# Layer 0 of a two-part transformer kernel: one gather of 8 KB rows in place of two gathers of 4 KB rows, over six places

## The reference, cut to what matters

```
def one(args):                      # a block of 128 tokens
    hh, ee, gg = args               # h, expert indices [128,128], gates [128,128]
    a = jnp.einsum("tkd,td->tk", peer_down[ee], hh)
    act = gg * jax.nn.gelu(a)
    return jnp.einsum("tk,tkd->td", act, peer_up[ee])
```

## Time and profile before

| | |
|---|---|
| median of 3 runs | 3811.63 us (3804.46 to 3811.77) |
| profiled execution, its own time | 3813.63 us |
| its span, first to last instruction | 3811.8 us |
| PE / DVE / ACT / POOL busy | 80% / 64% / 25% / 32% |
| bytes moved by DMA | 1156.88 MB, mean 304 GB/s |
| gathers (queue q0) | 805.39 MB |

### The profile page before, as it was taken

One profiled execution on the slowest core, in us unless ns is written; L12 is line 12 of the kernel. 1 busy time (PEld: TensorE's weight loads), 2 busy tenths in 40 slices (PEclk: granted clock), 3 DMA queues, 4 the chain that ended last, 5 costly groups with the idle time before them and its releaser, 6 DMA issues.

```text
span 3811.8 us, 42583 instructions
## 1 busy us (share of the span) xinstructions
PE 3054.7 (80%) x15018; PEld 1920.9 (50%) x15018; DVE 2452.1 (64%) x5511; ACT 969.7 (25%) x2143; POOL 1229.4 (32%) x1309
## 2 busy tenths in 40 slices
PE   6899776778775766676788877777798899999899
PEld 2487432333341221232256433323597789897798
DVE  3444888565578786555456887776565866565564
ACT  1432111220111111111131111112233543334433
POOL 0001566565567666666402333333100000000000
PEclk8999987888887887888789999999999999999999
DMA  7665999999999999999728999999654145454354
GB/s 301 260 253 218 385 408 397 388 392 377 396 405 389 410 407 394 410 409 410 303 72 336 389 405 411 413 406 416 241 189 160 61 149 194 162 199 167 127 178 153
DMA packets 237314, 1156.88 MB, mean 304 GB/s; under 512 B 26961, under 2 KB 27729, under 8 KB 165970
## 3 DMA queue, kind: packets, MB, share of 16 engines
q0 software_dynamic: 184320, 805.39, 52.9%
q1 hardware_dynamic: 52818, 349.25, 24.9%
HBM read 1153.49 MB, written 1.05 MB: 303 GB/s over the span
## 4 chain that ended last, share of the span: by engine, by line
PE 43%; DMA 26%; DVE 16%; POOL 7%; issue 5%; ACT 2%; SPq 0%; DVEq 0%; ACTq 0%; POOLq 0%
DMA rows<-in_peer_up,diag 13%; PE ps L1272 9%; PE ps L1273 9%; PE ps L1274 9%; POOL rows L2814 7%; DMA rows<-in_peer_down,idx 5%; DMA h_ctx<-in_peer,idx 4%; PE ps L1210 4%; PE ps L1175 4%; DMA rows<-in_peer,idx 3%; DVE rows L2324 3%; PE ps L883 1%; DVE shared L2557 1%; PE ps L1126 1%; DVE rows L2290 1%
## 5 line engine op out<-in xcount | busy, mean ns | idle before, releaser
L1210 PE MATMUL ps<-rows,diag 128*32 128x512 f32 x2048 | 589.0, 760 | 397.9 <-DMA rows<-in_peer_up,diag 392.8
L2324 DVE CUSTOM_DVE_ANT_0 rows<-rows,ps 128x1024 f32<-128x1024 f32 x512 | 614.4, 1219 | 348.9 <-DMA rows<-in_peer_down,idx 334.7
L2814 POOL DMA_INDIRECT rows<-in_peer_down,idx x512 | 487.9, 953 | 648.6 <-DVE gates L2277 364.4
L2814 POOL DMA_INDIRECT rows<-in_peer_up,diag x512 | 482.4, 942 | 251.1 <-DVE a L2324 140.7
L1210 PEld LDWEIGHTS ps<-rows,diag 128*32 128x32 f32 x2048 | 82.1, 120 | 866.1 <-DMA rows<-in_peer_up,diag 839.0
L1272 PE MATMUL ps<-hT_hi,w_hi 128*128 128x256 f32 x1792 | 508.6, 284 | 8.9 <-DVE hT_lo L2469 8.9
L1273 PE MATMUL ps<-hT_hi,w_lo 128*128 128x256 f32 x1792 | 508.8, 284 | 0.0
L1274 PE MATMUL ps<-hT_lo,w_hi 128*128 128x256 f32 x1792 | 507.8, 283 | 0.0
L2874 POOL TENSOR_TENSOR ss<-nwt,minus_half 128x1 f32<-128x1 f32 x24 | 13.2, 549 | 1097.5 <-DVE nwt L2009 1097.5
L1272 PEld LDWEIGHTS ps<-hT_hi,w_hi 128*128 128x128 f32 x1792 | 343.3, 192 | 14.4 <-issue 14.3
L2459 DVE TENSOR_TENSOR w_lo<-wring,w_hi 128x2048 fp32r<-128x2048 f32 x120 | 274.6, 2291 | 114.8 <-ACT w_hi L1852 113.5
(11 more groups left out here) (342 smaller groups left out, 4847.0 us busy)
## 6 DMA issues: line engine op xcount, KB each, us to landing
wring<-in_wgu SPq DMA_DIRECT2D x66, 1024.0 KB, 4.9
wring<-in_wdn SPq DMA_DIRECT2D x33, 1024.0 KB, 4.9
wring<-in_wG SPq DMA_DIRECT2D x32, 1024.0 KB, 7.9
wring<-in_wmod SPq DMA_DIRECT2D x28, 1024.0 KB, 8.1
wring<-in_wpq SPq DMA_DIRECT2D x24, 1024.0 KB, 8.0
rows<-in_wgu SPq DMA_DIRECT2D x22, 1024.0 KB, 4.9
rows<-in_wmod SPq DMA_DIRECT2D x20, 1024.0 KB, 7.8
rows<-in_wdn SPq DMA_DIRECT2D x11, 1024.0 KB, 4.9
```

The lines of the kernel that those rows point to most:

```text
L1210: ins = pe.matmul(ps[qd:qd + QUAD, UPB + half, :], quad_w[:, j, :], rows[:, j, half * 512:(half + 1) * 512], start=(first and j < QUADS), ...
L2324: dve.tensor_tensor_reduce(out=rows[:, j, :], in0=rows[:, j, :], in1=h_ps, scale=1.0, scalar=0.0, op0=ALU.mult, op1=ALU.add, accum_out=a8[ ...
L2814: pool.indirect_dma_start(out=rows[:, j, :], out_offset=None, in_=table, in_offset=bass.IndirectOffsetOnAxis(ap=of[:, g * GROUP + j:g * GR ...
```

## The change

- Layer 0 gathers pairs: a new table `peer0` has the down and the up row of an expert side by side (8 KB). One indirect DMA brings 128 such rows (1 MB), all in moved order. 128 gathers a tile instead of 256.
- They go through `SPREAD_PLACES = 6` places of 1 MB: the four of `rows`, `lent` (the context's residual tile `x[1]` up to gather 166, then a part of `kvmem`), and the third place of `wring`. The weight ring keeps two places until layer 0's gathers are over; `ctx` is loaded a second time (1 MB) once gather 166 is used.
- A gather takes 4 experts of 32 tokens of one quarter j of the tile. So the down product needs h with the quarter's 32 tokens repeated four times: `spread_h` on PE writes it, 8 matmuls each time the quarter or the set changes (48 times in all). ACT no longer copies h for layer 0.
- GELU is done gather by gather on ACT (`spread_diag`): five small activations and the scaled identity. The group instructions on DVE, `move` on PE and the copies go. The gates are brought to moved order along with the indices, in `moved`.
- Up products go to column groups j and j+2, j fixed in a quarter.
- On PE a slot (4 gathers) now mixes side products and ups: `between()` stands before each side product and, after every few, does the slot's next up. PE's side products have 4 banks instead of 3.
- The first set is moved before the gathers begin, and every gather waits for `moved`.

```
+def spread_gathers(t):
+    return [(TOP * h0 + QUADS * s + j, j, n) for n, (h0, h1) in enumerate(SETS[t]) for j in range(QUADS) for s in range(TOP * (h1 - h0) // QUADS)]
+def new_quarter(n):
+    return n % P == 0 or SPREADS[n][1:] != SPREADS[n - 1][1:]
...
-        s = ... min(range(SLOTS + ROW_SLOTS if n in middle else SLOTS), ...)
+        s = ... min(range(SLOTS + ROW_SLOTS if n in middle else SLOTS - 1 if n < narrow else SLOTS), ...)
...
+        def spread_place(n):
+            k = n % SPREAD_PLACES
+            return both[k] if k < HALF else lent[n > LENT] if k == HALF else wring[:, SLOTS - 1, :]
...  PE
+            def between():
+                pieces[0] += 1
+                if pieces[0] >= 4 and next_up[0] < last_up[0]:
+                    ups_to(next_up[0] + 1)
+            def spread_h(n):
+                ...  pe.wait_ge(down_done, n)
+                one_of = ident[:, QUAD * j:QUAD * (j + 1)]
+                for half in range(2):
+                    for i in range(QUADS):
+                        ins = pe.matmul(h_ps[qd:qd + QUAD, half * 512:(half + 1) * 512], one_of, h[...][:, t, half * 512:(half + 1) * 512], ...)
+            def spread_up(n):
+                pe.wait_ge(diag_ready, n + 1)
+                for half in range(2):
+                    qd = QUAD * ((j + 2 * half) % QUADS)
+                    ins = pe.matmul(ps[qd:qd + QUAD, UPB + half, :], quad_w[:, n % GROUP, :], spread_place(n)[:, D + half * 512:D + (half + 1) * 512], ...)
+            gather, each half:
+                    last_up[0] = n + HALF - 1
+                    run_stages(stages)
+                    ups_to(n + HALF - 1)
+                    if n + HALF < len(SPREADS) and new_quarter(n + HALF):
+                        spread_h(n + HALF)
+                    ups_to(n + HALF)
...  ACT
+            def spread_diag(n):
+                act.wait_ge(down_done, n + 1)
+                act.activation(sq, a, ACT.Square, scale=GELU_A ** 0.5)
+                act.activation(weight, a, ACT.Copy, scale=gates_moved[t][:, col:col + 1])
+                act.activation(inner, sq, ACT.Identity, scale=a, bias=a)
+                act.activation(th, inner, ACT.Tanh, scale=GELU_C)
+                act.activation(act_, th, ACT.Identity, scale=weight, bias=weight)
+                act.activation(quad_w[:, c, :], quad_id, ACT.Copy, scale=act_)
+            gather, each half: 4 x spread_diag, then the side stages
...  DVE
+            def spread_down(n):
+                if new_quarter(n):
+                    dve.wait_ge(h_spread, ...)
+                dve.wait_ge(row_in[k], 16 * (n // SPREAD_PLACES + 1))
+                dve.tensor_tensor_reduce(out=down, in0=down, in1=h_ps, ..., accum_out=a8[:, c:c + 1])
+            gather, each half: 4 x spread_down, then the side stages
...  POOL
+                if n >= SPREAD_PLACES:
+                    pool.wait_ge(upp_done, n - SPREAD_PLACES + 1)
+                pool.indirect_dma_start(out=spread_place(n), in_=A["peer0"], in_offset=idx_moved[t][:, col:col + 1])
```

More of the change, by code:

```diff
@@ L134, in during @@
     for t in range(TT):
-        n, mine = 0, slots[t * 2 * GROUPS:(t + 1) * 2 * GROUPS]
-        while n < GROUPS:
-            m = n + 1
-            if r != "x1" and not mine[2 * n] and not mine[2 * n + 1]:
-                while m < GROUPS and not mine[2 * m] and not mine[2 * m + 1]:
-                    m += 1
-            out.append(("gather", r, t, n, m, mine[2 * n], mine[2 * n + 1]))
-            n = m
+        mine = slots[t * 2 * GROUPS:(t + 1) * 2 * GROUPS]
+        for n in range(GROUPS):
+            out.append(("gather", r, t, n, mine[2 * n], mine[2 * n + 1]))
         if (r, t) == ("x1", 0):
@@ L417 @@
 ORDER = with_parts(order())
-STAGES = [st for e in ORDER for st in (e[5] + e[6] if e[0] == "gather" else [e])]
+STAGES = [st for e in ORDER for st in (e[4] + e[5] if e[0] == "gather" else [e])]
 def parted_chunks():
@@ L1229, in gather @@
-                if beside_a or beside_b:
-                    group(n0, beside_a)
-                else:
-                    groups(pe, n0, n1, group)
-                run_stages(beside_b)
-                if n1 == GROUPS and G + 1 not in JOINED:
-                    move(GROUPS - 1)
-                    up(GROUPS - 1, last=True)
+                        if i == 2 * PAIRS - 2:
+                            both_ups(i + 1)
+                        continue
+                    n = P * G + HALF * (2 * n0 + part_)
@@ L2304, in both_downs @@
                     residual("x1", 0)
-            def gather(run, t, n0, n1, beside_a, beside_b):
-                s = RUNS[run][0]
+            def spread_down(n):
+                if n % P == 2 and n > P:
+                    sum_of(*GATHERS[n // P - 1])
+                    residual(*GATHERS[n // P - 1])
+                c, k = n % GROUP, n % SPREAD_PLACES
+                if new_quarter(n):
+                    dve.wait_ge(h_spread, len([m for m in range(n + 1) if new_quarter(m)]))
+                dve.wait_ge(row_in[k], 16 * (n // SPREAD_PLACES + 1))
+                down = spread_place(n)[:, 0:D]
+                dve.tensor_tensor_reduce(out=down, in0=down, in1=h_ps, scale=1.0, scalar=0.0,
+                                         op0=ALU.mult, op1=ALU.add, accum_out=a8[:, c:c + 1]).then_inc(down_done, 1)
@@ L2350, in group @@
-                def group(n, stages_a=(), stages_b=()):
-                    first = is_group(n, 0)
-                    down(n, first)
-                    run_stages(stages_a)
-                    act_of(n, first)
-                    run_stages(stages_b)
-                if beside_a or beside_b:
-                    group(n0, beside_a, beside_b)
-                else:
-                    groups(dve, n0, n1, group)
+                    else:
+                        n = P * G + HALF * (2 * n0 + part_)
+                        for k in range(n, n + HALF):
+                            spread_down(k)
@@ L2861, in gather_both @@
                                             in_offset=bass.IndirectOffsetOnAxis(ap=idx[t][:, k:k + 1], axis=0)).then_inc(both_in[c], 16)
-            for run, t in GATHERS:
-                if run != "x1":
-                    gather(run, t)
+            for n in range(len(SPREADS)):
+                gather_spread(n)
             pool.wait_ge(upp_done, 4 * P)
```

335 lines of the change are left out of this document (142 added, 193 removed).

## The result

| | before | after |
|---|---|---|
| median | 3810.27 us (4 runs, 3804.46 to 3811.77) | 3850.41 us (4 runs, 3838.83 to 3853.65) |
| profiled execution, its span | 3811.8 | 3837.0 |
| first gather to last up of layer 0 | 364.9 to 1878.7, 1513.8 | 367.4 to 1924.9, 1557.5 |
| from there to x1's first gather | 145.0 | 144.6 |
| x1's first gather to the end (the rest) | 1788.1 | 1767.5 |

The changed kernel is slower, by 1.0103 [1.0078, 1.0127]; 3780 with a range of 3742 to 3845 was forecast. The stretch grew by 43.7 us, and the rest, in which no side stage was rewritten, became 20.6 us shorter. The profiled execution was the fastest of its four; two more profiles of the same code have stretches of 1574.4 and 1563.5 us, so differences under some 17 us between single profiles tell nothing.

The account below looks back on a forecast made before the run. Layer 0's stretch was taken as bound by DMA transfers; 371 + 1275 + 158 + 10 + 22 + 6 + 4 = 1846 us for the last up against 1878.7, 33 us less, giving 3780 us, range 3742 to 3845.

Parts of the forecast that it names:

- Start: Layer 0's first gather, behind moving all the first set's indices: 3 us later, at 368 (0 to 6); bytes from about 371.
- Transfers: Layer 0 stretch: 536.9 MB of gathers at 421 GB/s take 1275 us, the other 65.0 MB at 411 take 158 us.
- The six places: Layer 0's gather places: a turn may take 17.2 us; 9.1 outside plus 5.4 landing is 14.5, so transfers decide.
- rival B: Six places too few in layer 0, PE waiting inside side stages: turn 18.2 us, +50, so 3862 us; chance 0.17.
- ACT: Six ACT instructions a layer 0 gather: 1.3 us (1.25 to 1.84), 666 us added, about 770 of 1460 busy, no bound.
- spread_h: PE's 8 matmuls repeating h, 48 times: 1.8 us each, hidden, or next down waits 2 to 4 us within slack.
- DVE's slots: Layer 0 slots with routing pieces and four downs, 11.5 us, nearly level with DMA: 10 us added (0 to 25).
- PE's dense slots: Some 24 layer 0 slots with pq or gate stages: 13.4 us against 12.5 of DMA, 22 us added (0 to 60).
- Ring of two: Weight ring with two places in layer 0: just enough, except PE standing in the Fourier branch; 6 us in all.
- The rest as before: The program after layer 0's last up was taken to keep its time.
- End: Behind layer 0's last landing: down, ACT, up and hand-overs take 4 us, where 1.1 stood.
- The stated sign of error: The forecast as a whole is wrong if first gather to last up of layer 0 is longer than 1500 us.

Follow-up runs that it names:

- all three out: Changed kernel with h spread once a tile, four-head routing pieces split over two slots, and GELU left out (wrong numbers): 3782.72 us, 0.9938 [0.9920, 0.9956].

## Why the prediction was wrong, point by point

- *Start*: right. First gather at 367.4, 368 forecast.
- *Transfers*: the rate was nearly right where rows are asked for in time (416 to 419 GB/s, 421 forecast), but the mean is 388, since DMA's share is 0.96 and many windows dip. This is the consequence of the next point, not a cause: from 400 to 1880 us the share is 0.98, 0.96, 0.94 and 0.90 in the kernels with stretches of 1499.7, 1557.5, 1595.8 and 1651.9 us.
- *The six places*, the step that failed. The turn at its least was put at 9.4 us with a landing of 5.4, and 9.1 + 5.4 = 14.5 us was held against 17.2. The landing taken was the shortest of a row. Under load the median landing is 9.3 us, and the wait outside the transfer is 8.95, almost the 9.1 that layer 1 showed. Their sum, 18.25 us, is rival B's 18.2 and not the 14.5 that let the transfers decide. The sentence against B, that a landing of 8.4 us is mostly queueing and shrinks, was true only in part: with five places it shrinks by 1.1 us, not by what is lacking, and where the wait outside falls (no GELU, all three out) the landing grows again to 10.5 and 11.0.
- *Rival B*, priced at 3862 with a stretch of 1553: right in its place and its stretch (1557.5). Its time came out 12 lower because the rest is shorter. That places are too few is shown by the run that takes one away (+98 us) and by DMA's share. The way B gave for it, PE's stops inside a side stage, is shown only in part: adding one cost 75 us or more, but without the stops of the alternation the kernel is 35 us slower, and with the ups in front of them 16 slower. How much each wait of the turn is worth stays open.
- *ACT*: 1.3 us a gather forecast, range to 1.84; 1.76 us busy and a pitch of 1.57. "Not a bound" was right (871 of 1558 us busy), but the chain's length inside a turn is worth up to 37 us, and it stood in the sum at nothing.
- *spread_h*: its length was right (1.8 forecast, 1.92 measured); "the next down waits 2 to 4 us, within a place's slack" was wrong: up to 10.9 us and 133 in all, of which 15 to 32 us reach the end.
- *DVE's slots*, 10 us: the size fits what the split of the long pieces gave (4 to 21). The price of one such piece, put at 1.5 us, was not measured: the window at 680 us recovers with the split, the hole at 1480 doesn't.
- *PE's dense slots*, 22 us: probably too much. The dense window at 1040 us runs at 419 GB/s with PE at 39.27 of 40, and at 421 with PE busy throughout when the three terms are out, so changes between side products and ups cost nothing that shows there. But two windows, at 400 (333 GB/s, PE 37.78) and 920 us (389, PE 37.48), meet the sign that was stated for an error in this step; with the three terms out they run at 390 and 410, so part of their loss at least is not PE's work. The alternation itself, counted at nothing, earns 35 us.
- *Ring of two*, 6 us: 13.0 us of PE's waits, none of which comes back with a ring of three beside five places.
- *The rest as before*: wrong by 20.6 us, in the kernel's favour.
- *End*: within the 144.6 us to x1's first gather nothing changed.

The stretch was forecast at 1478 us. Taking out the three terms that were mis-sized or left out (ACT's chain, the wait for h, the long pieces) brings it from 1557.5 to 1499.7; the 22 us that remain were not separated, and holes like that at 1450 us are among them. The stated sign of error, a stretch above 1500 us, came true. And the sign of the whole depends on the chip, which neither the profile of before nor the forecast could show.

## What to carry to other kernels

Work out a place's turn with the median landing of rows under load and with every wait behind side stages, and hold it against places times pace before letting the transfers decide; here that turn came to 18.25 us, against 17.2, and cost more than a row faster by 2% brought. Where engines feed each other through a short ring, a small instruction put into the loop (ACT's chain, a wait for h) is paid for though its engine is half idle. Don't expect every stop to be worth its length: a stop put into PE's side work was paid in full here, but moving PE's work to take stops away made the kernel slower twice. Compare such kernels on more than one chip before calling one the faster.

## What the runs showed of the hardware that was not expected

- The kernel before took 3803 to 3815 us in four comparisons and 3866 to 3910 in two on other chips; the changed kernel did not move (3838 to 3860 in three comparisons, one of them on such a chip). There, in the one profile taken, PE is idle 179 us with no releaser in the profile.
- Side products and ups that alternate in different tilings of the array (128*128 and 128*32 in the timeline) follow each other without a gap that shows: 1.05 us for an up between them, as for a lone one, and 419 GB/s with PE at 39.27 of 40 us.
- ACT's instructions on 128x1 take 195 ns with a constant scale, 280 with a scale from memory and 373 to 387 with scale and bias from memory.
